# A two-part attention input: key RMS factors as token columns, and the rotary half swap as a DMA

## The chip, the cores and the metric

The kernel runs on one core of one Trainium2 chip. The metric is the device time in microseconds of that core for one execution. The time before is 2725.86 us, the median of 3 runs (2725.54 to 2731.17).

## What is computed

A latent sequence of 512 tokens and a context of 256 tokens, width 1024, go through four blocks in fp32: a hybrid block (mLSTM and short convolution) with an MLP, an attention block with an MLP, and two more blocks of pooling, spatial gating and a gated feed-forward. The change is in the input of the attention block, which is, cut to what matters:

```python
px = hx @ w_in                                   # hx: 512 latent tokens, hc: 256 context tokens
qx = apply_axial_rope(rms_norm(heads(px[..., :nq], 16), q_g), cos, sin)
kx, vx = kv(px[..., nq:])                        # kv: k = rms_norm(heads(k, 4), k_g), v as it is
kx = apply_axial_rope(kx, cos, sin)
kc, vc = kv(hc @ w_in[:, nq:])
k_all = concatenate([kc, kx]);  v_all = concatenate([vc, vx])      # 768 keys, 4 heads of 64

def rms_norm(x, g):  return x * rsqrt(mean(x * x, axis=-1) + EPS) * g
def _rotate_half(part, cs, sn):                  # of the first and of the second 32 channels of a head
    p1, p2 = part[..., :16], part[..., 16:]
    return concatenate([p1 * cs - p2 * sn, p2 * cs + p1 * sn])
```

## The kernel before

Activations lie channel-major: 128 channels on the partitions (two heads of 64), tokens along the free axis, NT = 768 = NC + NX = 256 context + 512 latent. Weights come as a stream of tiles, 128 partitions by 1024 columns (512 KB each). Tile t goes through four buffers (t % 4): SP issues its load once tile t - 4 is used (`load`, line 351), ACT writes the upper part `Whi` (`split_hi`, line 977), DVE the rest `Wlo` (`split_lo`, line 1465). `product` on TensorE (lines 417 to 430) waits for `Wlo`, and for the PSUM bank G[t % 2] to be freed by the evacuation of tile t - 2, then runs 8 times 3 matmuls for each part of the tokens; tiles of keys and values cover all 768 tokens, those of the queries the 512 latent ones.

The attention input has 12 tiles (t = 0 to 11 from T_ATT): two of values, two of keys (n = 0, 1), eight of queries (n = 2 to 9, n = t - 2). Each engine has its own written-out loop over t (TensorE 797, ACT 1299, DVE 2045), and within a loop everything runs in program order. ACT and DVE both begin step t with the split of tile t + 2.

- Keys: ACT copies the product to T (1317) and squares it (1321). TensorE multiplies all 768 tokens by a block of ones (`k_stats`, 771), which puts the sum of squares of a head on each of its channels. ACT takes the root over 128x768 (1332), DVE the reciprocal over 128x768 (`k_finish`, 2025), then normalizes to QN (2026) and copies the context part to AK (2029).
- Queries: ACT squares from PSUM (1324) and copies to T with the gain (1326). `q_stats` (780) puts the sums into columns of B4, a column for each head and 128 tokens; their root (1335) and reciprocal QR (2063) are taken once for all queries, and QR enters the softmax as its scale.
- Rotation: `qk_rotate` (784 to 795) on TensorE multiplies the latent part by the constant matrix `rotate`, which swaps the halves of 16 channels and sets the sign, into B6. `qk_turn` (2031 to 2041) on DVE forms x * cos (2038), swapped x * sin (2040) and their sum (2041) into AK or AQ, and counts `qk_ready`. T has two buffers: ACT may write that of tile n once `qk_ready` shows that n - 2 is turned (1315).

Behind the loop TensorE runs `scores_of(0)` (831), DVE takes `top(0)`, `top(1)` (2070), ACT exponentiates (`weigh`, 1344), and TensorE runs the next scores and `turn_probs` (847), which waits for `qk_ready` 10. `spread_sums` (857) shows the form of matmul that spreads a token column over 64 partitions.

Of the kernel before, what the change touches and what calls it, by code (L numbers as in the profile page):

```python
# [7 lines left out]
ALU = mybir.AluOpType  # L8
ACT = mybir.ActivationFunctionType
AX = mybir.AxisListType  # L10
# [91 lines left out]
def build(nc, xin, cvec, wstream, adaw, firstw, vecs_d, consts_d, rope_d, poolw_d, sguw_d, rows_d, out):  # L102
    ctx = ExitStack()
    with ctx:
# [78 lines left out]
        QR = sb("QR", [P, 64], where=att)  # L183
        p5 = ExitStack()
# [3 lines left out]
        RT = sb("RT", [P, NX], where=p5)  # L188
        p5.close()
# [47 lines left out]
        def ps(bank, a, b):  # L237
# [31 lines left out]
        qk_sq, qk_stat, qk_std, qk_n, rot_done, qk_ready, qr_ready, qg_ready = map(  # L269
            sem, ("qk_sq", "qk_stat", "qk_std", "qk_n", "rot_done", "qk_ready", "qr_ready", "qg_ready"))  # L270
# [65 lines left out]
        def _(sp):  # L336
# [41 lines left out]
            stream(T_ATT + 4, T_S)  # L378
# [37 lines left out]
        def _(pe):  # L416
# [349 lines left out]
            def k_stats(n):  # L766

                pe.wait_ge(qk_sq, n + 1)
                wait(pe, qk_std, n)
                for a, b in parts(FULL):  # L770
                    last = pe.matmul(ps(B4, a, b), blockones, SQ[:, n % 2, a:b], start=True, stop=True)
                last.then_inc(qk_stat, 1)

# [10 lines left out]
            def qk_rotate(n):  # L784

                if n < 2:
                    pe.wait_ge(qk_n, n + 1)
                else:
                    freed(pe, At(T_ATT + 2 + n))
                wait(pe, qk_ready, n - 1)  # L790
                if n == 0:
                    pe.wait_ge(turn_used, 6)
                src_ = QN if n < 2 else T
                pe.matmul(B6[:, NX * (n % 2):NX * (n % 2 + 1)], rotate, src_[:, n % 2, NC:NT], start=True,
                          stop=True).then_inc(rot_done, 1)

            for t in range(N_ATT):
                rng = FULL if t < 4 else LAT
                if t == 0:
                    first_products(At(T_ATT), src, FULL, src_ready, At(8 * S_N2))  # L800
                elif t > 1:
                    product(At(T_ATT + t), src, rng)
                if 1 <= t < 3:
                    turn(4 + t - 1, 0, TT)
                if 3 <= t < 5:
                    k_stats(t - 3)
                if t >= 5:
                    q_stats(t - 3)
                if 4 <= t < 6:
                    qk_rotate(t - 4)  # L810
                if t >= 5:
                    qk_rotate(t - 3)
            q_stats(9)
            qk_rotate(9)
# [157 lines left out]
        def _(act):  # L972
# [326 lines left out]
            for t in range(N_ATT):  # L1299
# [7 lines left out]
                else:  # L1307
# [20 lines left out]
                    if 1 <= n < 3:  # L1328
                        a, b = FULL
                        act.wait_ge(qk_stat, n)  # L1330
                        wait(act, qk_n, n - 1)
                        act.activation(RS[:, a:b], ps(B4, a, b), ACT.Sqrt, scale=1.0 / HD,
                                       bias=VEC[:, VEC_AT["eps"]:VEC_AT["eps"] + 1]).then_inc(qk_std, 1)
# [120 lines left out]
        def _(dve):  # L1454
# [566 lines left out]

            def k_finish(n):

                dve.wait_ge(qk_std, n + 1)
                link(dve.reciprocal(RS[:, :], RS[:, :]))
                dve.scalar_tensor_tensor(out=QN[:, n, :], in0=T[:, n, 0:NT], scalar=vec("k_g"), in1=RS[:, :],
                                         op0=ALU.mult, op1=ALU.mult).then_inc(qk_n, 1)
                dve.wait_ge(qk_n, n + 1)
                dve.tensor_copy(AK[:, n, 0:NC], QN[:, n, 0:NC])

            def qk_turn(n):
                wait(dve, qk_ready, n)
                if n < 2:
                    dst, x_ = AK[:, n, NC:NT], QN[:, n, NC:NT]
                else:
                    dst, x_ = AQ[:, n - 2, :], T[:, n % 2, NC:NT]
                    freed(dve, At(T_ATT + 2 + n))
                link(dve.tensor_tensor(RT[:, :], x_, ROPE[:, 0, :], ALU.mult))
                dve.wait_ge(rot_done, n + 1)
                link(dve.tensor_tensor(dst, B6[:, NX * (n % 2):NX * (n % 2 + 1)], ROPE[:, 1, :], ALU.mult))  # L2040
                dve.tensor_tensor(dst, dst, RT[:, :], ALU.add).then_inc(qk_ready, 1)


            dve.tensor_scalar(small[:, 0:1], vec("q_g"), HD ** -0.5, None, ALU.mult).then_inc(qg_ready, 1)
            for t in range(N_ATT):
                split_lo(At(T_ATT + t + 2))
                if 1 <= t < 3:
                    n = 4 + t - 1
                    dve.wait_ge(turned, n + 1)
                    dve.tensor_copy(AV[:, :, (n - 4) * P:(n - 3) * P],  # L2050
                                    B6[:, 0:NT].rearrange("p (i c) -> p i c", c=P)).then_inc(turn_used, 1)
                if t == 4:
                    dve.wait_ge(late_in, 16)
                if 3 <= t < 5:
                    if t == 4:
                        qk_turn(0)
                    k_finish(t - 3)
                if t == 5:
                    qk_turn(1)
                if t >= 5:  # L2060
                    qk_turn(t - 3)
            dve.wait_ge(qk_std, 3)
            dve.reciprocal(QR[:, :], QR[:, :]).then_inc(qr_ready, 1)
            qk_turn(9)
# [28 lines left out]
            top(1)  # L2093
            for n in range(2 * AH):
# [365 lines left out]
```

## Time and profile before

The trace is of one execution, taken by the hardware profiler.

| | before |
|---|---|
| median of the runs | 2725.86 us |
| the profiled execution, its device time | 2728.78 us |
| its span in the trace | 2727.1 us |
| TensorE busy | 2624.9 us (96%) |
| VectorE busy | 1631.4 us (60%) |
| ScalarE busy | 958.7 us (35%) |
| GpSimd busy | 96.3 us (4%) |
| mean granted TensorE clock | 0.981 |

Times in the trace count from the start of its span. Matmul records overlap, since matmuls are pipelined: what one costs is the distance between starts, not its own length. An fp32 matmul shows as two records. The chain of work that ended last is followed back from the last instruction: each piece is what released the next one. The granted clock is a share of 2.4 GHz: 1.00 is 2.4 GHz, 0.50 is 1.2 GHz.

### The profile page before, as it was taken

Reading aid. Unit: us, or ns where it says so; the run is one execution under the profiler, and the core shown is the slowest. Engines: PE = TensorE matmul, PEld = TensorE weight load, DVE = VectorE, ACT = ScalarE, POOL = GpSimd, SP = SyncE. Lnnn points to the kernel's source line nnn. Section 1 sums busy time; section 2 is a strip of 40 time slices with the busy share of each in tenths; the row PEclk is TensorE's granted clock in tenths of the full one; section 3 lists DMA queues with packets and bytes.
Section 4 is the critical chain, followed back from the end, with each engine's and each line's share of the span. In section 5 each row is a group of like instructions: output and inputs, shape, how many; then the busy total and the mean of one; then the engine's idle time right before and its main releaser. Section 6 shows DMA issues by size and latency. Waiting matters only on the chain.

```text
span 2727.1 us, 35868 instructions
## 1 busy us (share of the span) xinstructions
PE 2624.9 (96%) x13720; PEld 2169.0 (80%) x13720; DVE 1631.4 (60%) x2534; ACT 958.7 (35%) x1405; POOL 96.3 (4%) x185
## 2 busy tenths in 40 slices
PE   7999998999999989899999999989999989899997
PEld 6888887888888877568788888878888778788886
DVE  4877646454546546664755565676566766644446
ACT  2323523222212232674422233353232453532224
POOL 0000000000000000000000000000001000000000
PEclk9999998999999989999999999999999999999998
DMA  6342322333334312001445554234546522233332
GB/s 242 124 139 86 116 78 70 109 108 108 111 110 130 118 49 68 1 1 55 155 147 162 162 187 126 77 101 145 164 149 190 164 81 80 76 93 95 98 94 85
DMA packets 82634, 303.43 MB, mean 111 GB/s; under 512 B 9168, under 2 KB 11344, under 8 KB 81488
## 3 DMA queue, kind: packets, MB, share of 16 engines
q1 hardware_dynamic: 56448, 206.82, 24.0%
q0 software_dynamic: 26064, 94.91, 11.0%
q8 instruction: 85, 1.39, 0.2%
q14 instruction: 37, 0.30, 0.0%
HBM read 299.60 MB, written 2.10 MB: 111 GB/s over the span
## 4 chain that ended last, share of the span: by engine, by line
PE 53%; DVE 5%; ACT 2%; issue 1%; DMA 1%; SPq 0%; ACTq 0%; DVEq 0%
PE G L427 12%; PE G L428 12%; PE G L429 12%; PE G L454 3%; PE G L455 3%; PE G L456 3%; PE B L871 1%; PE G L831 1%; PE G L503 1%; PE G L505 1%; DVE X L1723 1%; PE G L504 1%; PE B L847 1%; DVE T L1720 1%; ACT PR L1344 1%
## 5 line engine op out<-in xcount | busy, mean ns | idle before, releaser
L977 ACT ACTIVATE Whi<-Wraw 128x1024 fp32r<-128x1024 f32 x357 | 374.9, 1051 | 492.3 <-DMA Wraw<-wstream_dram 467.3
L1465 DVE TENSOR_TENSOR Wlo<-Wraw,Whi 128x1024 fp32r<-128x1024 f32 x357 | 436.3, 1222 | 120.7 <-ACT Whi L977 120.1
L427 PE MATMUL G<-h_hi,Whi 128*128 128x512 f32 (+1 forms) x1040 | 372.8, 358 | 2.8 <-DVE Wlo L1465 2.8
L429 PE MATMUL G<-h_hi,Wlo 128*128 128x512 f32 (+1 forms) x1040 | 367.1, 353 | 0.0
L428 PE MATMUL G<-h_lo,Whi 128*128 128x512 f32 (+1 forms) x1040 | 366.9, 353 | 0.0
L427 PE MATMUL G<-hs_hi,Whi 128*128 128x512 f32 x768 | 307.2, 400 | 2.6 <-DVE Wlo L1465 1.7
L428 PE MATMUL G<-hs_lo,Whi 128*128 128x512 f32 x768 | 303.9, 396 | 0.0
L429 PE MATMUL G<-hs_hi,Wlo 128*128 128x512 f32 x768 | 303.8, 396 | 0.0
L429 PE MATMUL G<-hid_hi,Wlo 128*128 128x512 f32 (+1 forms) x792 | 290.8, 367 | 0.0
L427 PE MATMUL G<-hid_hi,Whi 128*128 128x512 f32 (+1 forms) x792 | 290.7, 367 | 0.0
L428 PE MATMUL G<-hid_lo,Whi 128*128 128x512 f32 (+1 forms) x792 | 290.5, 367 | 0.0
L427 PEld LDWEIGHTS G<-h_hi,Whi 128*128 128x128 f32 x1040 | 196.6, 189 | 37.8 <-issue 5.9
L1547 DVE SCALAR_TENSOR_TENSOR X<-G,MOD,X 128x256 f32<-128x256 f32 (+1 forms) x112 | 69.8, 653 | 259.9 <-PE G L429 197.9
L428 PEld LDWEIGHTS G<-h_lo,Whi 128*128 128x128 f32 x1040 | 196.5, 189 | 30.6 <-issue 2.2
L1480 DVE SCALAR_TENSOR_TENSOR Araw<-Araw,CB 128x1024 f32<-128x1024 f32 x180 | 219.0, 1219 | 2.9 <-DMA Araw<-adaw_dram 2.9
L429 PEld LDWEIGHTS G<-h_hi,Wlo 128*128 128x128 f32 x1040 | 196.3, 189 | 29.7
L427 PEld LDWEIGHTS G<-hs_hi,Whi 128*128 128x128 f32 x768 | 144.4, 188 | 38.7 <-DVE Wlo L1465 3.4
L428 PEld LDWEIGHTS G<-hs_lo,Whi 128*128 128x128 f32 x768 | 144.5, 188 | 35.4 <-issue 1.0
L429 PEld LDWEIGHTS G<-hs_hi,Wlo 128*128 128x128 f32 x768 | 144.3, 188 | 35.3
L428 PEld LDWEIGHTS G<-hid_lo,Whi 128*128 128x128 f32 x792 | 148.5, 188 | 27.6
L429 PEld LDWEIGHTS G<-hid_hi,Wlo 128*128 128x128 f32 x792 | 148.5, 188 | 27.5
L427 PEld LDWEIGHTS G<-hid_hi,Whi 128*128 128x128 f32 x792 | 148.6, 188 | 27.5
(387 smaller groups left out, 4397.2 us busy)
## 6 DMA issues: line engine op xcount, KB each, us to landing
Wraw<-wstream_dram SPq DMA_DIRECT2D x357, 512.0 KB, 3.7
Araw<-adaw_dram POOLq DMA_DIRECT2D x180, 512.0 KB, 4.0
FIRST<-firstw_dram SPq DMA_DIRECT2D x4, 1536.0 KB, 23.0
X<-xin_dram SPq DMA_DIRECT2D x4, 1536.0 KB, 11.3
out_dram<-X SPq DMA_DIRECT2D x16, 128.0 KB, 1.7
ROW<-rows_dram SPq DMA_DIRECT2D x2, 768.0 KB, 6.2
CB<-cvec_dram SPq DMA_DIRECT2D x2, 512.0 KB, 5.5
CB<-cvec_dram POOLq DMA_DIRECT2D x1, 512.0 KB, 4.5
```

The lines of the kernel that those rows point to most:

```text
L427: pe.matmul(o, wh, hi[:, a:b], start=(k == 0), stop=False)
L428: pe.matmul(o, wh, lo[:, a:b], start=False, stop=False)
L429: last = pe.matmul(o, wl, hi[:, a:b], start=False, stop=(k == kt - 1))
L454: pe.matmul(o, wh, hi[:, a:b], start=(nth == 0), stop=False)
L455: pe.matmul(o, wh, lo[:, a:b], start=False, stop=False)
L456: last = pe.matmul(o, wl, hi[:, a:b], start=False, stop=(nth == kt - 1))
L503: pe.matmul(o, wh, hi[:, a:b], start=first, stop=False)
L504: pe.matmul(o, wh, lo[:, a:b], start=False, stop=False)
L977: act.activation(Whi[:, t % 4, :], Wraw[:, t % 4, :], ACT.Copy).then_inc(w_hi, 1)
L1465: dve.tensor_tensor(Wlo[:, t % 4, :], Wraw[:, t % 4, :], Whi[:, t % 4, :].bitcast(F32), ALU.subtract).then_inc(w_lo, 1)
L1480: last = dve.scalar_tensor_tensor(out=products, in0=Araw[:, n % 2, :], scalar=1.0, in1=CB[:, v, :], op0=ALU.mult, op1=ALU.mult, accum_out=o)
L1547: last = dve.scalar_tensor_tensor(out=X[:, m, a:b], in0=ps(G[t % 2], a, b), scalar=MOD[:, par, v, gate * 8 + m:gate * 8 + m + 1], in1=X[:, ...
```

## The change

1. `k_stats` puts the sums of squares of the keys into columns of B4 (12 columns for each key tile: 6 blocks of 128 tokens by 2 heads), as `q_stats` does. ACT's root and DVE's reciprocal then work on 128x12 (KR). A new `k_spread` on TensorE spreads the columns over the channels of their head by 12 small matmuls with the identity into B6, one step later; DVE's `k_finish` reads them there.
2. `qk_rotate` is gone. SP copies the latent part of T (or QN) to SWAP by eight DMAs of 16 partitions each, a group g from the group g ^ 16. The sign is put into the sine table once (`signed_sine`).
3. The DMAs are written into SP's program between the loads of the weight tiles, with their waits, and DVE's `qk_turn` runs one step later (n = t - 4 instead of n = t - 3); the last, `qk_turn(9)`, comes behind `top(0)` and `top(1)`.

```diff
+            def swap_halves(n):
+                if n < 2:
+                    sp.wait_ge(qk_n, n + 1)
+                else:
+                    sp.wait_ge(tile_free[(T_ATT + 2 + n) % 2], (T_ATT + 2 + n) // 2 + 1)
+                wait(sp, qk_ready, n - 1)
+                x_ = (QN if n < 2 else T)[:, n % 2, NC:NT]
+                for g in range(0, P, 16):
+                    sp.dma_start(SWAP[g:g + 16, n % 2, :], x_[g ^ 16:(g ^ 16) + 16, :]).then_inc(swapped[n % 2], 16)
+
+            for t in range(4, N_ATT + 3):
+                load(At(T_ATT + t))
+                for n in {7: (0,), 8: (1, 2), 9: (3, 4)}.get(t, (t - 5,) if t > 9 else ()):
+                    swap_halves(n)
+            stream(T_ATT + N_ATT + 3, T_S)
...
 def k_stats(n):
-                for a, b in parts(FULL):
-                    last = pe.matmul(ps(B4, a, b), blockones, SQ[:, n % 2, a:b], start=True, stop=True)
+                for i in range(TT):
+                    at = 64 + 2 * TT * n + 2 * i
+                    last = pe.matmul(B4[:, at:at + 2], SQ[:, n % 2, blk(i)], blockones[:, 0:P:HD], start=True, stop=True)
+            def k_spread(n):
+                pe.wait_ge(kr_ready, n + 1)
...
+                for i in range(TT):
+                    for e in range(2):
+                        last = pe.matmul(ps(B6, i * P, (i + 1) * P)[HD * e:HD * (e + 1), :],
+                                         KR[:, n, 2 * i + e:2 * i + e + 1].to_broadcast([P, HD]), ident, start=True,
+                                         stop=True)
+                last.then_inc(k_spread_done, 1)
...
-                pe.matmul(B6[:, NX * (n % 2):NX * (n % 2 + 1)], rotate, src_[:, n % 2, NC:NT], start=True,
-                          stop=True).then_inc(rot_done, 1)
...
+                if 4 <= t < 6:
+                    k_spread(t - 4)
                 if 3 <= t < 5:
                     k_stats(t - 3)
                 if t >= 5:
                     q_stats(t - 3)
-                if 4 <= t < 6:
-                    qk_rotate(t - 4)
-                if t >= 5:
-                    qk_rotate(t - 3)
             q_stats(9)
-            qk_rotate(9)
...
+            def k_invert(n):
+                dve.wait_ge(qk_std, n + 1)
+                dve.reciprocal(KR[:, n, :], KR[:, n, :]).then_inc(kr_ready, 1)
 def k_finish(n):
-                dve.wait_ge(qk_std, n + 1)
-                link(dve.reciprocal(RS[:, :], RS[:, :]))
-                dve.scalar_tensor_tensor(out=QN[:, n, :], in0=T[:, n, 0:NT], scalar=vec("k_g"), in1=RS[:, :],
-                                         op0=ALU.mult, op1=ALU.mult).then_inc(qk_n, 1)
-                dve.wait_ge(qk_n, n + 1)
-                dve.tensor_copy(AK[:, n, 0:NC], QN[:, n, 0:NC])
+                dve.wait_ge(k_spread_done, n + 1)
+                for dst, a, b in ((AK[:, n, 0:NC], 0, NC), (QN[:, n, NC:NT], NC, NT)):
+                    last = dve.scalar_tensor_tensor(out=dst, in0=T[:, n, a:b], scalar=vec("k_g"), in1=ps(B6, a, b),
+                                                    op0=ALU.mult, op1=ALU.mult)
+                last.then_inc(qk_n, 1)
...
-                dve.wait_ge(rot_done, n + 1)
-                link(dve.tensor_tensor(dst, B6[:, NX * (n % 2):NX * (n % 2 + 1)], ROPE[:, 1, :], ALU.mult))
+                dve.wait_ge(swapped[n % 2], 128 * (n // 2 + 1))
+                link(dve.tensor_tensor(dst, SWAP[:, n % 2, :], ROPE[:, 1, :], ALU.mult))
...
+            def signed_sine():
+                dve.wait_ge(late_in, 16)
+                link(dve.tensor_reduce(small[:, 1:2], rotate, AX.X, ALU.add, negate=True))
+                link(dve.tensor_scalar(ROPE[:, 1, :], ROPE[:, 1, :], small[:, 1:2], None, ALU.mult))
...
-                if t == 4:
-                    dve.wait_ge(late_in, 16)
+                if t == 2:
+                    signed_sine()
+                if 4 <= t < 6:
+                    k_finish(t - 4)
                 if 3 <= t < 5:
-                    if t == 4:
-                        qk_turn(0)
-                    k_finish(t - 3)
-                if t == 5:
-                    qk_turn(1)
-                if t >= 5:
-                    qk_turn(t - 3)
+                    k_invert(t - 3)
+                if t in (5, 6):
+                    qk_turn(t - 5)
+                if t >= 6:
+                    qk_turn(t - 4)
+            qk_turn(8)
             dve.wait_ge(qk_std, 3)
             dve.reciprocal(QR[:, :], QR[:, :]).then_inc(qr_ready, 1)
-            qk_turn(9)
...
             top(0)
             top(1)
+            qk_turn(9)
```

## Rows read from the trace of the kernel before

**Rows 1.** The page: chain that ended last, share of the span by engine.

```profile
PE 53%; DVE 5%; ACT 2%; issue 1%; DMA 1%; SPq 0%; ACTq 0%; DVEq 0%
```

**Rows 2.** Windows: us, each engine's busy time (instructions), PEclk, DMA share, GB/s.

```profile
1036.00:1038.00 2.00, 0.84 (x9) 0.75 (x7) 1.97 (x2) 0.00 (x0) 0.00 (x0) 1.00 0.37 55
1038.00:1040.00 2.00, 1.24 (x2) 0.73 (x3) 1.97 (x3) 1.21 (x3) 0.00 (x0) 0.50 0.52 207
1092.00:1094.00 2.00, 0.00 (x0) 0.00 (x0) 1.80 (x4) 1.16 (x3) 0.00 (x0) 1.00 0.00 0
```

**Rows 3.** Chain that ended last, at the second key tile: start us, us, what.

```profile
1032.79 4.87 DVE RS L2025
...
1037.69 1.03 DVE QN L2026
...
1038.76 3.78 PE B L794 x4
1042.54 0.43 PE G L427
```

**Rows 4.** Timeline of TensorE: start us, us, engine line op, tiles, xcount [idle before].

```profile
1020.56 1.45 PE L771 MATMUL B<-SQ,CON 128*128 128x256 f32 x4
...
1078.49 0.95 PE L780 MATMUL B<-CON,SQ 128*128 128x2 f32 x8
1079.30 1.10 PE L794 MATMUL B<-T,CON 128*128 128x512 f32 x2
1079.84 0.80 PE L427 MATMUL G<-h_hi,Whi 128*128 128x512 f32 x1
1080.48 0.40 PE L428 MATMUL G<-h_lo,Whi 128*128 128x512 f32 x1
...
1085.85 0.95 PE L780 MATMUL B<-CON,SQ 128*128 128x2 f32 x8
```

**Rows 5.** Waits between 1020 and 1092: engine, line <- releaser: total us, times, longest.

```profile
PE B L794 <- DVE QN L2026: 2.4, 2, 1.9
```

**Rows 6.** Timeline of DVE from the last rotation into the attention.

```profile
1089.66 0.63 DVE L2038 TENSOR_TENSOR RT<-T,ROPE 128x512 f32<-128x512 f32 x1
...
1091.66 0.95 DVE L2070 TENSOR_REDUCE NM<-G 128x1 f32<-128x768 f32 x1
...
1095.63 0.96 DVE L2070 TENSOR_REDUCE NM<-B 128x1 f32<-128x768 f32 x1 [1.76 <-PE G L831]
```

**Rows 7.** Timeline of TensorE: a spread of eight token columns.

```profile
1116.46 1.04 PE L857 MATMUL B<-CON,ZR 128*64 128x128 f32 x16
```

**Rows 8.** Timeline of SP: DMAs that it issues back to back.

```profile
4.32 0.62 SPq L346 DMA_DIRECT2D X<-xin_dram  x1
...
2202.62 0.33 SPq L384 DMA_DIRECT2D POW<-poolw_dram  x1
2202.99 0.43 SPq L385 DMA_DIRECT2D SW<-sguw_dram  x1
```

**Rows 9.** The page, DMA issues: xcount, KB each, median us from issue to landing.

```profile
Wraw<-wstream_dram SPq DMA_DIRECT2D x357, 512.0 KB, 3.7
...
out_dram<-X SPq DMA_DIRECT2D x16, 128.0 KB, 1.7
...
POW<-poolw_dram SPq DMA_DIRECT2D x2, 256.0 KB, 2.6
SW<-sguw_dram SPq DMA_DIRECT2D x2, 256.0 KB, 3.0
```

**Rows 10.** Timelines of ACT and DVE in a query step.

```profile
1078.69 0.60 ACT L1324 ACTIVATE SQ<-G 128x512 f32<-128x512 f32 x1 [5.23 <-PE G L429]
...
1079.76 1.06 ACT L977 ACTIVATE Whi<-Wraw 128x1024 fp32r<-128x1024 f32 x1
...
1081.85 1.22 DVE L1465 TENSOR_TENSOR Wlo<-Wraw,Whi 128x1024 fp32r<-128x1024 f32 x1
1082.99 0.68 DVE L2038 TENSOR_TENSOR RT<-T,ROPE 128x512 f32<-128x512 f32 x1
```

More of the change, by code:

```diff
@@ L183, in build @@
         QR = sb("QR", [P, 64], where=att)
+        KR = sb("KR", [P, 2, 2 * TT], where=att)
         p5 = ExitStack()
@@ L188, in build @@
         RT = sb("RT", [P, NX], where=p5)
+        SWAP = sb("SWAP", [P, 2, NX], where=p5)
         p5.close()
@@ L268, in build @@
         hsq2_ready, hidhi_ready = map(sem, ("hsq2_ready", "hidhi_ready"))
-        qk_sq, qk_stat, qk_std, qk_n, rot_done, qk_ready, qr_ready, qg_ready = map(
-            sem, ("qk_sq", "qk_stat", "qk_std", "qk_n", "rot_done", "qk_ready", "qr_ready", "qg_ready"))
+        qk_sq, qk_stat, qk_std, qk_n, qk_ready, qr_ready, qg_ready, kr_ready, k_spread_done = map(
+            sem, ("qk_sq", "qk_stat", "qk_std", "qk_n", "qk_ready", "qr_ready", "qg_ready", "kr_ready",
+                  "k_spread_done"))
+        swapped = [sem(f"swapped{i}") for i in range(2)]
         as_done, amax_ready, aexp_done, at_done, at_used_act, at_used_dve, apv_done, ao_hi_ready = map(
@@ L377, in _ @@
             sp.dma_start(ROPE[:, :, :], rope_d).then_inc(late_in, 16)
-            stream(T_ATT + 4, T_S)
+            def swap_halves(n):
[12 more added lines that the diff above has]
+            stream(T_ATT + N_ATT + 3, T_S)
             for l in range(2):
@@ L769, in k_stats @@
                 wait(pe, qk_std, n)
-                for a, b in parts(FULL):
-                    last = pe.matmul(ps(B4, a, b), blockones, SQ[:, n % 2, a:b], start=True, stop=True)
+                for i in range(TT):
+                    at = 64 + 2 * TT * n + 2 * i
+                    last = pe.matmul(B4[:, at:at + 2], SQ[:, n % 2, blk(i)], blockones[:, 0:P:HD], start=True, stop=True)
                 last.then_inc(qk_stat, 1)
+            def k_spread(n):
+                pe.wait_ge(kr_ready, n + 1)
+                if n == 0:
+                    pe.wait_ge(turn_used, 6)
+                wait(pe, qk_n, n)
+                for i in range(TT):
[4 more added lines that the diff above has]
+                last.then_inc(k_spread_done, 1)
             def q_stats(n):
@@ L782, in q_stats @@
                 last.then_inc(qk_stat, 1)
[L784 to L793, printed above, removed]
-                pe.matmul(B6[:, NX * (n % 2):NX * (n % 2 + 1)], rotate, src_[:, n % 2, NC:NT], start=True,
-                          stop=True).then_inc(rot_done, 1)
             for t in range(N_ATT):
@@ L1328, in _ @@
                     if 1 <= n < 3:
-                        a, b = FULL
                         act.wait_ge(qk_stat, n)
-                        wait(act, qk_n, n - 1)
-                        act.activation(RS[:, a:b], ps(B4, a, b), ACT.Sqrt, scale=1.0 / HD,
+                        at = 64 + 2 * TT * (n - 1)
+                        act.activation(KR[:, n - 1, :], B4[:, at:at + 2 * TT], ACT.Sqrt, scale=1.0 / HD,
                                        bias=VEC[:, VEC_AT["eps"]:VEC_AT["eps"] + 1]).then_inc(qk_std, 1)
@@ L2034, in qk_turn @@
                     dst, x_ = AK[:, n, NC:NT], QN[:, n, NC:NT]
+                    dve.wait_ge(qk_n, n + 1)
                 else:
```

## The prediction, made before the changed kernel was seen

> **What bounds the kernel now.** I read the page first. TensorE is the largest term of the chain that ended last [rows 1], so only what lies on TensorE's path counts, and the question is what the attention input costs there. The stretch runs from 1020.56, where the product of the second key tile ends and `k_stats` begins, to 1085.85, where the last query product ends [rows 4]: 65.29 us. Behind it, until DVE's third maximum at 1095.63 [rows 6], the chain goes through DVE. From there on nothing is touched by the change.
>
> The timeline of TensorE gives the price of each piece in a query step, as distances of starts [rows 4]. 23 product matmuls, from the second of a tile at 1080.48 to the next `q_stats` at 1085.85, take 5.37 us, 0.233 each, so a product of 24 takes 5.60. `q_stats` takes 0.81 (1078.49 to 1079.30). `qk_rotate` takes 0.54 to the next start, and the first product matmul behind it takes 0.64 where 0.233 is normal, so a rotation costs 0.54 + 0.41 = 0.95.
>
> The chain [rows 3] shows why the keys cost more. The reciprocal over 128x768 (4.87) and the normalization (1.03) on DVE released the rotation of the key, for which TensorE sat idle 2.4 us in two waits, 1.9 of them in the second [rows 5]. Behind the second wait the windows show the granted clock at 0.50, 1.2 GHz, having been 1.00 while TensorE was busy only 0.84 of 2.00 us [rows 2]. Two rotations took 3.78 instead of 1.9, and the first product matmul behind them 0.43 instead of 0.233 [rows 3]; six ran at that pace. The fall cost 1.9 + 1.2 = 3.1.
>
> **The change part by part.**
>
> *Rotations off TensorE.* Eight stood before 1085.85 and two behind, 0.95 each. In the stretch that is 7.6; the two waits add 2.4 and the clock 3.1. Removed: 13.1.
>
> *`k_stats` as columns.* 6 blocks against 4 in `q_stats`: 0.81 x 6/4 = 1.22. Before, it took about 0.9 + 0.4 for the late first product matmul, 1.3. Two of them: gain 0.2.
>
> *`k_spread`, new.* The nearest row is the same form with 8 matmuls. Its record has 1.04 us [rows 7], part of which overlaps the next, as the 0.95 of `q_stats` stands for a distance of 0.81 [rows 4]. That is 0.90 to 1.04 for 8, 1.35 to 1.56 for 12; I take 1.47, twice 2.94. If they were free the time would be 2.9 lower, which is the bound below; above, I take 12 at 0.25 (one product matmul's pace), 3.0 each. I keep 1.47, since the form is the same. Its input is ready: root and reciprocal of 128x12 follow 1.3 us after `k_stats`, and a product of 5.6 us hides them. Without that cover they would cost these 1.3.
>
> *Restart behind a small matmul.* No row shows a product directly behind `q_stats`. Between 0 and the 0.41 behind a rotation; I take 0.1, since the 0.41 follows 512 moving columns and these have 2. Eight products: 0.8.
>
> TensorE's own path from 1020.56 is then 8 x 5.7 + 2 x 1.22 + 2 x 1.47 + 6 x 0.81 = 55.8, and the last product ends at 1076.4, 9.4 us earlier, provided that nobody makes it wait.
>
> *DVE.* The two long reciprocals and the copies go, and the two halves of `k_finish` cost what one 128x768 costs (1.03 [rows 3]), plus 0.2. `signed_sine` (a 128x128 sum and a 128x512 product, about 1 us by the 0.68 of a 128x512 [rows 10]) lies in an idle time of DVE ahead of the next split and costs nothing; without that cover the split would move 1 us and still have a whole product in hand.
>
> *SP, the part that decides.* Each tile now has eight DMAs and their waits in front of the next weight load. The first of a sequence takes 0.33 and the next starts 0.37 behind it; that next one takes 0.43, with the same gap 0.47; the longest has 0.62, with the gap 0.66 [rows 8]. All those have 128 partitions, these 16, so the bound below is open (0.05, if it goes by descriptors) and above 0.66. I take 0.40, near the lower of the pair, so 3.2 for a tile. For landing, the eight together are 256 KB: between 1.7 (128 KB) and 2.6 (256 KB) [rows 9]; I take 2.0 from the last issue.
>
> Behind the waiting SP stand the weight loads: load n + 6 is issued only when tile n is evacuated and swapped. On the price of an issue the Trainium skill ("DMA: Bandwidth & Descriptors", Anatomy of one DMA) has about 50 ns for the dispatch by a sequencer. No row of this case shows an issue under 0.33, and the row decides. By the skill's figure the loads would not be late and the time would be that of the second case below.
>
> I follow the new loop through. Let E(n) be the time when ACT has evacuated query tile n. A cycle over two tiles is: swap(n) issued 3.2, load 3.7 [rows 9], `split_hi` 1.1 (1.06 [rows 10]), `split_lo` 1.15 (1081.85 to 1082.99), `qk_turn` 2.0 (1089.66 to 1091.66 [rows 6]), ACT's square and copy 1.2 (1.07 from 1078.69 to 1079.76 and 0.1 for the semaphore [rows 10]), 0.1 for a semaphore: 12.45. TensorE needs 2 x (5.7 + 0.81) = 13.0 for two tiles. So it holds, with 0.5 to spare, but starts late. Product 4 ends at 1020.6 + 1.2 + 5.7 = 1027.5; `k_spread(0)` and `k_stats(1)` take 2.7, product 5 ends at 1035.9 and `k_spread(1)` at 1037.3; `k_finish(1)` takes 1.2 and ends at 1038.6. Then come the swap of n = 1 until 1041.9, that of n = 2 until 1045.1 and load 9 behind them (landing 1048.8). The swap of n = 2 lands at 1046.7 (7 issues and 2.0 behind its start), DVE has turned n = 2 1.3 later, at 1048.0, and with ACT's 1.2 E(4) is 1049.2. E(5) lies 5.4 behind it (`split_hi`, `split_lo`, `qk_turn`, ACT: 1.1 + 1.15 + 2.0 + 1.2), and from there every second one follows in 12.4: E(6) = 1061.6, E(8) = 1074.0, and on the odd side E(5) = 1054.6, E(7) = 1067.0, E(9) = 1079.4. TensorE wants E(4) by 1051.2, E(5) by 1057.7, E(6) by 1064.2, E(7) by 1070.7, so no product waits. But `q_stats(9)` wants the last square, at 1078.8 instead of 1077.2. TensorE idles 1.7 us.
>
> *The end.* `scores_of(0)` starts at 1079.7, its first result is there 1.6 later, and `top(0)` runs at 1081.3 instead of 1091.66. The last swap is issued from 1079.5 and lands at 1084.3; `top(1)` ends at 1083.4, so `qk_turn(9)` ends at 1085.7. Before, the third maximum came 3.97 behind the first [rows 6], which would be 1085.3. So it now starts at 1085.7, and the gain is 1095.63 - 1085.7 = 9.9 us. `turn_probs` waits for the same `qk_ready` and moves by the same.
>
> **The rivals.**
>
> *The cover holds whole.* If an issue takes well under 0.37, SP is not in the cycle, the first maximum is at 1076.4 + 1.6 + 1.6 = 1079.6, and the third, behind the turn, at 1083.7 to 1084.0. Gain 11.6 to 11.9, up to 12.5 if restarts are free: 2713.4 to 2714.3. For it: 16 descriptors instead of 128. Against: the 0.33 of every single issue.
>
> *SP becomes the bound.* The issue time enters the chain to the end five times eight, so the gain is 9.9 - 40 x (issue - 0.40): at 0.47 7.1, at 0.66 -0.5 (2726.4). From 0.65 on the change gives nothing.
>
> *The other side: the pieces land one by one.* POW and SW, issued 0.37 apart, land 0.8 apart (2.6 and 3.0 after issue) [rows 8, 9]. If each small DMA occupied the queue that long, a swap would take 6.4 instead of 3.2 and the load behind it would wait with it, which acts like an issue time of 0.80: 9.9 - 16 = -6.1, 2732.0. It decides from about 0.78 (5.5 us slower). For it stands the Trainium skill (same page, Rules for kernel authors): "Two transfers to disjoint partition halves" serialize, and under 64 KB a transfer is mostly overhead; these have 32 KB. Against it: those 0.8 us were for 256 KB of data, eight times as much, so little of it can be a fixed share.
>
> *The clock falls again.* TensorE idles 1.7 us at the end of the input, after sparse matmuls, as it did before the fall [rows 2]. In the other stretch, 1092 to 1094, it did nothing and the clock stayed at 1.00. If it falls: 3.1, gain 6.8, 2719.1.
>
> **How the numbers follow.** The profiled execution ran 2728.78 with a span of 2727.1; less 9.9 its span is 2717.2. Against the median it is 2725.9 - 9.9 = 2716.0, since the profiled run stood 2.9 above it and the gain is in one stage. Chances: forecast (issue 0.37 to 0.47, 2714.8 to 2718.8) 0.50; cover whole 0.15; clock 0.10; SP the bound with 0.47 to 0.70 (2718.8 to 2728) 0.15; one by one 0.10. About 0.2%, 5.5 us, is what a measurement can tell. Faster takes the first three but for 0.02 and a third of the fourth: 0.77, taken as 0.75. Slower 0.10, same 0.15. The range goes from the whole cover, 2713.5, to the zero point of SP as the bound, 2726; it leaves out the one-by-one case and the ends of the others.
>
> **What would show it.** TensorE: `q_stats` followed by L427 in under 0.3 us beyond 0.81, no rotation, no idle time and clock 1.00 between 1020 and 1077; `k_spread` 1.3 to 1.6. SP: eight issues 0.37 to 0.47 apart, landing under 3 us. The last product ends at 1076 to 1077, then an idle time of 1 to 3 us before the last `q_stats`; first maximum at 1081, third at 1085 to 1086. The forecast is wrong if products wait for `Wlo` or the PSUM bank, if a load lands after ACT asks for it by more than in the cycle above, or if the clock is at 0.50 anywhere in the stretch.

## The result, and the profile after

| | before | after |
|---|---|---|
| median of 20 runs each, same chip | 2727.26 us | 2733.05 us |
| ratio, with its 95% interval | | 1.0021 [1.0014, 1.0028] |
| the profiled execution, its device time | 2728.78 us | 2734.78 us |
| its span | 2727.1 us | 2733.1 us |

The change makes the kernel 5.7 us slower (2727.26 x 0.0021), where 9.9 us faster was forecast. The page of after: all engines together have less to do than before, and the time went up.

```profile
span 2733.1 us, 36001 instructions
PE 2622.0 (96%) x13764; PEld 2170.9 (79%) x13764; DVE 1623.6 (59%) x2536; ACT 957.8 (35%) x1405; POOL 96.1 (4%) x185
SWAP<-T SPq DMA_DIRECT2D x64, 32.0 KB, 2.0
```

TensorE is busy 2.9 us less, VectorE 7.8. The timeline of TensorE in after answers [rows 4, 5] (L792 is `k_stats`, L803 `k_spread`, L814 `q_stats`, L447 the first matmul of a product, L849 `scores_of`):

```profile
1021.87 1.40 PE L792 MATMUL B<-CON,SQ 128*128 128x2 f32 x12
1023.12 0.47 PE L447 MATMUL G<-h_hi,Whi 128*128 128x512 f32 x1
...
1028.89 1.53 PE L803 MATMUL B<-CON,KR 128*64 128x128 f32 x24
1030.35 1.50 PE L792 MATMUL B<-CON,SQ 128*128 128x2 f32 x12
...
1053.84 1.05 PE L814 MATMUL B<-CON,SQ 128*128 128x2 f32 x8 [1.70 <-ACT SQ L1342]
...
1070.30 1.87 PE L814 MATMUL B<-CON,SQ 128*128 128x2 f32 x8 [3.24 <-ACT SQ L1342]
1072.03 0.77 PE L447 MATMUL G<-h_hi,Whi 128*128 128x512 f32 x1
...
1086.46 0.95 PE L814 MATMUL B<-CON,SQ 128*128 128x2 f32 x8
1091.38 1.86 PE L814 MATMUL B<-CON,SQ 128*128 128x2 f32 x8 [3.97 <-ACT SQ L1342]
1093.18 2.93 PE L849 MATMUL G<-AK,AQ 64*128 64x512 f32 x8
```

Counted from the end of the second key product (1020.56 before, 1021.87 after; the 1.3 us between lie ahead of the change), the last product ended at +65.29 and now ends at 1086.46, +64.59. Of the forecast 9.4 us only 0.7 came. `q_stats` waits three times for its square, 1.70, 3.24 and 3.97 us. The first two lie ahead of the end of the last product, and behind the second the clock was at half: from 1070.30 to the next `q_stats` at 1080.00 it took 9.70 us, where the same step takes 6.46 at full clock (1080.00 to 1086.46). These 4.9 + 3.2 us, with some 0.4 of slower starts behind waits, are what the last product lost against the +55.98 that the kernels without waits reach below. The third wait comes behind it. The third maximum, which closed the stretch at +75.07 [rows 6], now starts at 1101.56, +79.69: 4.6 us later, and the span is 6.0 longer, 1.3 of it from ahead. So the loss lies in this stretch: 0.7 us gained up to the last product, 5.3 lost between it and the third maximum (15.1 us instead of 9.8).

Who made the square late? The timelines of ACT and DVE ahead of the wait at 1070.30:

```profile
1065.19 1.06 ACT L995 ACTIVATE Whi<-Wraw 128x1024 fp32r<-128x1024 f32 x1 [4.80 <-DMA Wraw<-wstream_dram]
1069.65 0.60 ACT L1342 ACTIVATE SQ<-G 128x512 f32<-128x512 f32 x1 [3.39 <-DVE AQ L2063]
1066.29 1.23 DVE L1482 TENSOR_TENSOR Wlo<-Wraw,Whi 128x1024 fp32r<-128x1024 f32 x1 [7.15 <-ACT Whi L995]
1067.43 0.69 DVE L2060 TENSOR_TENSOR RT<-T,ROPE 128x512 f32<-128x512 f32 x1
```

Each step stands behind the one before: a weight tile lands, ACT splits it at 1065.19 after 4.80 us of waiting, DVE's half of the split begins at 1066.29, the turn of tile 4 behind it in program order at 1067.43, and only then is a buffer of T free for tile 6, so its square starts at 1069.65. TensorE names the square, ACT names the turn, but the first of the chain is a load. The timeline of SP in after says why the load was late (L392 are the swaps, L355 the weight loads):

```profile
1031.64 5.31 SPq L392 DMA_DIRECT2D SWAP<-QN  x8
1037.00 0.57 SPq L355 DMA_DIRECT2D Wraw<-wstream_dram  x1
1040.22 4.94 SPq L392 DMA_DIRECT2D SWAP<-QN  x8
1045.28 4.94 SPq L392 DMA_DIRECT2D SWAP<-T  x8
1050.26 0.58 SPq L355 DMA_DIRECT2D Wraw<-wstream_dram  x1
1050.94 9.98 SPq L392 DMA_DIRECT2D SWAP<-T  x16
1060.97 0.58 SPq L355 DMA_DIRECT2D Wraw<-wstream_dram  x1
1061.65 6.07 SPq L392 DMA_DIRECT2D SWAP<-T  x8
1067.76 0.58 SPq L355 DMA_DIRECT2D Wraw<-wstream_dram  x1
```

From 1040.22 to 1067.76 SP does nothing but issue: five swaps of eight DMAs and two loads between them. A swap takes 5.0 us, 0.63 for each DMA: 0.59 in the median and a gap of 0.04. One issue took 1.64, which is why one swap shows as 6.07. The tile SWAP in after:

```profile
L392 SPq DMA_DIRECT2D SWAP<-T x64: 507/589/1640, 1045.3 to 1096.3; - x64
DMA to landing us min/median/max: 1.9/2.0/3.7
```

The granted clock fell twice, after the second and the third wait. Windows of after, to be held against [rows 2]:

```profile
1066.00:1070.00 4.00, 1.06 (x5) 0.53 (x3) 3.21 (x4) 0.61 (x2) 0.00 (x0) 1.00 0.37 75
1072.00:1074.00 2.00, 2.00 (x6) 1.61 (x7) 1.24 (x2) 0.72 (x1) 0.00 (x0) 0.50 0.25 57
1088.00:1090.00 2.00, 0.00 (x0) 0.00 (x0) 1.93 (x4) 0.00 (x0) 0.00 (x0) 1.00 0.23 52
1094.00:1096.00 2.00, 2.00 (x8) 0.67 (x4) 0.18 (x1) 0.90 (x1) 0.00 (x0) 0.50 0.27 67
```

### The profile page after: what moved, and what is told of

It reads as the page before. It is cut to its first block, busy times and chain, and to the rows that moved or that the text cites. A ratio compares the mean times of both kernels' runs of the same rounds, so it can differ in the third digit from the quotient of the medians.

```text
span 2733.1 us, 36001 instructions
## 1 busy us (share of the span) xinstructions
PE 2622.0 (96%) x13764; PEld 2170.9 (79%) x13764; DVE 1623.6 (59%) x2536; ACT 957.8 (35%) x1405; POOL 96.1 (4%) x185
## 3 DMA queue, kind: packets, MB, share of 16 engines
q0 software_dynamic: 26064, 94.91, 11.2%
## 4 chain that ended last, share of the span: by engine, by line
PE 87%; DVE 6%; ACT 3%; issue 2%; DMA 1%; SPq 1%; DVEq 0%; ACTq 0%
PE G L447 20%; PE G L449 20%; PE G L448 20%; PE G L474 5%; PE G L475 5%; PE G L476 5%; PE B L640 2%; SPq L392 1%; PE G L849 1%; PE B L889 1%; PE G L523 1%; PE G L524 1%; PE G L525 1%; DVE X L1740 1%; PE B L865 1%
## 5 line engine op out<-in xcount | busy, mean ns | idle before, releaser
L447 PE MATMUL G<-h_hi,Whi 128*128 128x512 f32 (+1 forms) x1040 | 371.1, 357 | 2.8 <-DVE Wlo L1482 2.8
L447 PE MATMUL G<-hs_hi,Whi 128*128 128x512 f32 x768 | 306.4, 399 | 2.6 <-DVE Wlo L1482 1.7
L447 PE MATMUL G<-hid_hi,Whi 128*128 128x512 f32 (+1 forms) x792 | 290.6, 367 | 0.0
L447 PEld LDWEIGHTS G<-h_hi,Whi 128*128 128x128 f32 x1040 | 197.6, 190 | 35.6 <-issue 3.7
L447 PEld LDWEIGHTS G<-hs_hi,Whi 128*128 128x128 f32 x768 | 144.0, 187 | 38.7 <-DVE Wlo L1482 3.4
L447 PEld LDWEIGHTS G<-hid_hi,Whi 128*128 128x128 f32 x792 | 148.5, 188 | 27.5
```

The source lines that it names most:

```text
L447: pe.matmul(o, wh, hi[:, a:b], start=(k == 0), stop=False)
```

## The experiments

Two theories stood against each other. SP: the eight issues cost 0.63 us each and stand ahead of the next load, so their number and their place set the time. Clock: the time goes with the fall of TensorE's clock at the handover to the attention, whatever caused the waits. Beside them, the parts of the change were tried alone. The medians are of 20 runs for after, of 11 for e1, e2, e5, e9 and e10, and of 5 for the others. Local times below count from the end of the second key product, as above, and are of one profiled execution each. The last product's time is where it ends.

| kernel | median, us | before, same chip | ratio [95%] | last product | third maximum |
|---|---|---|---|---|---|
| before | | | | +65.29 | +75.07 |
| after | 2733.05 | 2727.26 | 1.0021 [1.0014, 1.0028] | +64.59 | +79.69 |
| e1_columns | 2731.68 | 2727.54 | 1.0015 [1.0005, 1.0024] | +61.99 | +79.21 |
| e2_load_first | 2723.55 | 2727.54 | 0.9987 [0.9978, 0.9996] | +57.94 | +71.27 |
| e3_four | 2718.12 | 2727.54 | 0.9965 [0.9951, 0.9978] | +55.98 | +66.15 |
| e4_one | 2717.78 | 2727.54 | 0.9965 [0.9952, 0.9979] | +55.98 | +63.68 |
| e5_columns_in_step | 2725.11 | 2728.74 | 0.9992 [0.9983, 1.0001] | +62.85 | +74.00 |
| e6_sixteen | 2781.16 | 2728.74 | 1.0194 [1.0180, 1.0208] | +93.46 | +124.23 |
| e7_four_first | 2716.60 | 2728.74 | 0.9959 [0.9945, 0.9972] | +55.98 | +64.22 |
| e8_four_first_busy | 2718.80 | 2728.74 | 0.9965 [0.9951, 0.9978] | +55.98 | +63.68 |
| e9_after_busy | 2732.01 | 2727.46 | 1.0017 [1.0008, 1.0026] | +61.69 | +77.54 |
| e10_rows_eight | 2731.22 | 2727.46 | 1.0016 [1.0007, 1.0025] | +62.26 | +78.68 |
| e11_rows_four_first | 2717.70 | 2727.46 | 0.9964 [0.9950, 0.9977] | +53.08 | +63.92 |
| e12_four_first_again | 2717.64 | 2727.46 | 0.9961 [0.9948, 0.9975] | +55.98 | +64.73 |
| e13_rows_busy | 2715.55 | 2728.31 | 0.9948 [0.9935, 0.9962] | +53.14 | +61.63 |
| e14_four_busy_again | 2718.20 | 2728.31 | 0.9960 [0.9946, 0.9973] | +55.98 | +63.67 |

**The columns alone.** The key factors as columns, with the rotation left on TensorE.

```diff
-            for t in range(4, N_ATT + 3):
-                load(At(T_ATT + t))
-                for n in {7: (0,), 8: (1, 2), 9: (3, 4)}.get(t, (t - 5,) if t > 9 else ()):
-                    swap_halves(n)
-            stream(T_ATT + N_ATT + 3, T_S)
+            stream(T_ATT + 4, T_S)
...
+            def qk_rotate(n):
...
+                pe.matmul(turned_half(n), rotate, src_[:, n % 2, NC:NT], start=True,
+                          stop=True).then_inc(rot_done, 1)
```

> Only the first part of the change: key factors as columns and their spread; the rotation stays a matmul on TensorE, one step later than before (n = t - 4), with the last turn behind the second maximum. Theory (the columns gain, the DMAs lose): the two waits for the key (2.4 us) and the clock's fall (3.1) go, two spreads of 1.46 come, one rotation moves behind the last product: 3.4 less up to the last product, 0.5 given back behind it, so 2.9 us faster than before. Rival (the sparse matmuls of the columns cost the clock or delay the key): 2 us or more slower than before.

The last product ended at +61.99, as expected, and yet the kernel is 4.1 us slower than before by the ratio, where 2.9 faster was expected. I had put each rotation one step later, to match after's turns. At the end that gives another wait, 2.26 us, and the last two rotations at half clock. Timeline of TensorE in e1_columns (L827 is the rotation):

```profile
1085.96 1.87 PE L815 MATMUL B<-CON,SQ 128*128 128x2 f32 x8 [2.26 <-ACT SQ L1360]
1087.69 3.76 PE L827 MATMUL B<-T,CON 128*128 128x512 f32 x4
```

So this run says nothing of the columns, but of the handover: 3.3 us saved in the products were lost there more than twice over. The next kernel puts the rotations of the later query tiles (n = 5 and up) back into the steps where before had them, and the last turn ahead of the first maximum. Against e1, on TensorE:

```diff
-                if t in (5, 6):
-                    qk_rotate(t - 5)
-                if t >= 6:
-                    qk_rotate(t - 4)
+                for n in {5: (0,), 6: (1, 2), 7: (3, 4)}.get(t, (t - 3,) if t > 7 else ()):
+                    qk_rotate(n)
```

> As e1, but with the rotations of the queries from the fifth on back in the step they had before (n = t - 3) and the last turn ahead of the first maximum, as before. In e1 the last square waited for the turn of tile 7, whose rotation stood behind the last product, and TensorE idled 2.3 us and fell to 1.2 GHz. Theory (the columns gain, e1 lost by its order at the end): 65.3 us up to the last product become 62.8, nothing is given back behind it: 2.5 us faster than before. Rival (the columns lose by themselves): 2 to 4 us slower than before, as e1.

The last product came at +62.85, as expected. By the ratio the gain is 2.2 us, of the expected size, though its interval reaches past 1. What the columns give here is that the key's long wait goes. In the profiled execution only 1.1 of the 2.4 us is left at the third maximum (+74.00 against +75.07): the third scores ran at half clock there, which had not been expected.

**Order of the load.** One change in SP's program against after: each load goes ahead of the swaps that it stood behind (from n = 5 on the load of tile n + 6 ahead of the swap of tile n).

```diff
-            for t in range(4, N_ATT + 3):
+            for t in range(4, 9):
                 load(At(T_ATT + t))
...
+            for n in range(5, 10):
+                if n + 6 < N_ATT + 3:
+                    load(At(T_ATT + n + 6))
+                swap_halves(n)
```

> The changed kernel with one thing moved in SP's program: the load of weight tile n + 6 stands ahead of the eight DMAs of query n instead of behind them. Theory (SP's issue time, 8 x 0.63 = 5.0 us, stands between the evacuation of tile n and load n + 6): the load leaves that cycle, the last query tile is evacuated about 9 us earlier than in the changed kernel, and the time is 3 to 4 us below that of before. Rival 1 (the landing of the small DMAs, or the turn one step later, sets the pace): within 1 us of the changed kernel, 5 to 6 above before.

As expected: 2723.55, 9.5 us below after by the medians (3.5 by the ratio below before), with the same DMAs. The swaps land as in after (2.0 us in the median) and the turns stand in the same step, so neither explains the difference. The order by itself doesn't tell SP's issue time from transfers that hold up a load behind them, but the load was hardly held there: in after ACT's split began 3.9 to 4.2 us after the issue of such a load, against a landing of 3.7 in the median before [rows 9].

**Number of issues.** The channels of a head are permuted on the host so that the partner lies 32 partitions away; four DMAs of 32 partitions then do the same swap. On the chip only the count that DVE waits for changes with it.

```diff
-                for g in range(0, P, 16):
-                    sp.dma_start(SWAP[g:g + 16, n % 2, :], x_[g ^ 16:(g ^ 16) + 16, :]) ...
+                for g in range(0, P, 32):
+                    sp.dma_start(SWAP[g:g + 32, n % 2, :], x_[g ^ 32:(g ^ 32) + 32, :]) ...
```

> The changed kernel with the channels of a head laid out so that the partner of a channel is 32 partitions away instead of 16: four DMAs of 32 partitions for a swap instead of eight of 16, same bytes, same place in SP's program. Theory (time goes by the number of issues, 0.63 each): 2.5 us for a swap instead of 5.0, less than the 3.7 up to which the load is in time, so TensorE waits nowhere and the gain against before is 11 to 12 us. Rival (an issue costs by its rows or bytes): 4 x 1.25, as slow as the changed kernel, 5 to 6 above before.

9.5 us faster than before by the ratio, short of the 11 to 12 expected, which the interval (6.0 to 13.4) still holds: the last `q_stats` waits 0.92 us, and the third scores run at half clock. With twice the bytes in each DMA the issue still takes 0.59, so a swap takes 2.4 us. The tile SWAP in e3_four:

```profile
L392 SPq DMA_DIRECT2D SWAP<-T x32: 507/590/595, 1040.9 to 1079.9; - x32
```

One DMA of 128 partitions, which leaves the half swap out (it copies only), shows what less than four would be worth.

```diff
+                sp.dma_start(SWAP[:, n % 2, :], x_).then_inc(swapped[n % 2], 16)
```

> The changed kernel with one DMA of 128 partitions in place of the eight. It copies each channel to its own place, so the half swap is left out and the rotated values are other ones; everything else is the same. Theory (number of issues): nothing left of SP's share; 11.5 to 12 us below before, hardly better than with four. Rival 1 (landing, 2.0 us, and the turn one step later): no gain from fewer issues, 5 to 6 above before.

The same time as with four, 9.5 and not the 11.5 to 12 expected, and an issue of 0.47. The tile SWAP in e4_one:

```profile
L391 SPq DMA_DIRECT2D SWAP<-T x8: 464/465/471, 1038.6 to 1075.5; - x8
```

And sixteen DMAs of 8 partitions, in the other direction.

```diff
+                for g in range(0, P, 8):
+                    sp.dma_start(SWAP[g:g + 8, n % 2, :], x_[g ^ 16:(g ^ 16) + 8, :]) ...
```

> The changed kernel with sixteen DMAs of 8 partitions for each swap: twice the issues, the same bytes. Theory (0.63 for each issue, SP is the bound): a swap takes 10 us of SP instead of 5, nine of them in a row with one load each: 9 x 5 = 45, less what SP idled in the changed kernel, about 39 above it and 44 above before, 2772. Rival 1 (time goes by bytes or by landing): within 2 us of the changed kernel. Rival 2 (the clock of TensorE is the main loss): under 10 above the changed kernel.

52.9 us slower than before by the ratio: 0.625 an issue, 10.7 a swap, and one `q_stats` that waits 16.27 us. That is 9 more than the 44 expected; about 5 of them are the issue, 0.665 with its gap instead of 0.63 (9 x 16 x 0.035), the rest I did not trace. The tile SWAP, and TensorE's timeline, in e6_sixteen:

```profile
L392 SPq DMA_DIRECT2D SWAP<-T x128: 624/625/652, 1052.1 to 1140.6; - x128
...
1066.35 1.87 PE L814 MATMUL B<-CON,SQ 128*128 128x2 f32 x8 [16.27 <-ACT SQ L1342]
```

One, four, eight and sixteen issues for each tile give -9.5, -9.5, +5.7 and +52.9 us by the ratios, and an issue takes 0.47 to 0.63 whatever it moves. With one and with four the last product ends at the same +55.98, so SP is not in the cycle; with eight and sixteen it is. Together with the order, that settles the cause for SP's issues. What an issue spends its time on, no run shows.

**Both mendings together.** Four DMAs and the load first; run twice.

```diff
+                if n + 6 < N_ATT + 3:
+                    load(At(T_ATT + n + 6))
+                swap_halves(n)
...
+                for g in range(0, P, 32):
```

> e3 and e2 together: four DMAs of 32 partitions and the load of tile n + 6 ahead of the swap of n. In e3 ACT still waited 2.5 us in all for weight loads and TensorE 0.9 for the last square. Theory (issue time and order are the whole loss): neither is left, the last product ends 56 us behind the key's product, gain against before 10 to 12 us. Rival (the rest of e3's loss lies in the turn one step later): as e3, 9 to 9.5.

> e7 once more, on the chip of e11, to compare the two: 10 to 12 us below before.

11.2 and 10.6 us faster than before by the ratios. TensorE waits for nothing up to the last product, at +55.98, and from n = 5 on the load of tile n + 6 no longer waits for the swap of tile n.

**The clock.** Dummy matmuls, which nobody reads, fill TensorE's waits: two behind the first scores in e8; in e9 the kernel after itself with 1, 3 and 6 ahead of three `q_stats` and 2 behind the scores.

```diff
+            for _ in range(2):
+                pe.matmul(B6[:, 0:NX], ident, CON[:, 0:NX], start=True, stop=True)
             for n in range(2 * AH):
```

> e7 with two matmuls (128x512 of constants by the identity, read by nobody) behind the first scores, where TensorE waits 2.5 us for ACT: about 1.9 us of work in an idle time. In e3 the granted clock was 0.50 for the next scores and transposes and the third maximum came 5.35 behind the first; in e4 it was 1.00 and 4.2. Theory (the idle time lets the clock fall): the clock stays at 1.00, third maximum 4.2 behind the first, and the time is 0 to 1.2 us below e7, since e7 falls only in some executions. Rival (the clock has nothing to do with it, or the extra matmuls delay the scores): equal to e7 or up to 1 us above.

```diff
+                fill({7: 1, 9: 3}.get(t, 0))
                 if t >= 5:
                     q_stats(t - 3)
+            fill(6)
             q_stats(9)
```

> The changed kernel with matmuls of constants that nobody reads (128x512, about 0.95 us each) where TensorE waited: 1 ahead of q_stats(4), 3 ahead of q_stats(6), 6 ahead of q_stats(9), 2 behind the first scores. It separates the price of the waits from that of the clock that fell behind them. Theory: the waits stay, since SP sets them; the fall between 1070 and 1077 (3.2 us) only moves into the last wait, but the one at the end (1.0 in q_stats, 1.4 in the scores, 1.2 to the third maximum) is on the path, so 2.5 to 3.5 us below the changed kernel, 2 to 3 above before. Rival (the clock costs nothing that SP has not already cost): equal to the changed kernel.

In e8 the clock stayed at 1.00 and the third maximum came 0.5 earlier than in e7. The time does not show it: the median is 2.2 us above that of e7, where 0 to 1.2 below was expected, and the five runs of e8 spread over 9.8 us. In e9 it stayed at 1.00 from 1020 to 1102, and the kernel is still slower than before, 4.6 us instead of 5.7. The expected gain of 2.5 to 3.5 over after was too high. The third maximum came at +77.54 rather than +79.69. The turn of the last tile then holds the path, and it hangs on SP, whose last swap starts at +69.81 in e9 and at +70.06 in after; TensorE waits for that turn. Timeline of TensorE in e9_after_busy (L873 is `turn_probs`):

```profile
1096.54 0.63 PE L873 MATMUL B<-CON,PR 128*128 128x128 f32 x4 [1.59 <-DVE AQ L2072]
```

The clock theory alone falls: with no fall at all four fifths of the loss remain (4.6 of 5.7), and even the lower end of its interval, 2.2 us, is a loss. How the loss splits in the medians is not sharp, since the intervals of e9 and after overlap; the local times carry it.

**The DMA part alone.** The key factors as rows again, as before had them, on top of after, and on top of the mended kernel.

```diff
-                for i in range(TT):
-                    last = pe.matmul(B4[:, at:at + 2], SQ[:, n % 2, blk(i)], blockones[:, 0:P:HD], start=True, stop=True)
+                for a, b in parts(FULL):
+                    last = pe.matmul(ps(B4, a, b), blockones, SQ[:, n % 2, a:b], start=True, stop=True)
...
-                    k_spread(t - 4)
```

> Only the second part of the change: the swap by eight DMAs as in the changed kernel, the key factors again over 128x768 rows with the 4.9 us reciprocals on DVE, no spread. Theory (SP is the bound, the columns only move when it starts): the second key is ready about 1.5 us earlier, SP's row of swaps starts that much earlier, so 4 to 5 us above before. Rival (the DMAs need the columns to pay): 8 us or more above before.

> e7 (four DMAs of 32 partitions, load ahead of the swap) with the key factors over rows again. Theory (with the rotation off TensorE nobody there waits for DVE's long reciprocals, and the two spreads are 2.9 us of TensorE for nothing): 2.5 to 3 us below e7, 13.5 to 14.5 below before. Rival (the reciprocals still delay the keys or the splits): level with e7 or above it.

With eight DMAs, 4.4 us slower than before, as expected: the loss is that of the DMAs, and the columns neither cause nor cure it. With four, the last product came 2.9 us earlier than in e12, as expected (55.98 - 53.08, the two `k_spread`), but the time did not: 2717.70 against 2717.64, and by the ratio 9.8 us below before instead of the 13.5 to 14.5 expected. Behind a wait of 0.65 the first scores ran at half clock, and the third maximum stood only 0.8 ahead. Timeline of TensorE and a window of e11_rows_four_first:

```profile
1076.03 2.38 PE L855 MATMUL G<-AK,AQ 64*128 64x512 f32 x6
...
1078.00:1082.00 4.00, 1.49 (x6) 0.64 (x6) 2.97 (x6) 1.88 (x3) 0.00 (x0) 0.50 0.51 164
```

If that is the reason, dummies in e11 should bring the 2.9 us out. The next kernel has rows, four DMAs, the load first and dummies (one ahead of the last `q_stats`, two behind the scores), and beside it the same with columns (e8 again):

```diff
+            fill(1)
             q_stats(9)
...
             scores_of(0)
+            fill(2)
```

> e11 with one matmul of constants ahead of q_stats(9) and two behind the first scores. In e11 the last product ended 53.1 us behind the key's (56.0 in e12), 2.9 earlier as expected, but its time was level with e12: the clock stood at 0.50 already in the first scores, where e12 still had 1.00. Theory (the clock took most of the 2.9): with the idle times filled the clock stays at 1.00, the third maximum comes 61 us behind the key's product instead of 63.9, and the time is 1.5 to 3 us below e11 and 12 to 13 below before. Rival (the last turn, or something else at the handover, holds it): third maximum at 63 to 64, time as e11.

> e8 once more, on the chip of e13: clock at 1.00 up to the third maximum, which comes 63.7 behind the key's product; 10 to 12 us below before. Theory: e13 is 2 to 3 below it.

e14 is as expected. In e13 the clock is 1.00 and the third maximum comes at 1082.98, +61.63, where 61 was expected; the gain is above the 12 to 13 expected. Window and timeline of DVE in e13_rows_busy:

```profile
1078.00:1082.00 4.00, 3.40 (x14) 1.42 (x12) 3.24 (x7) 2.87 (x5) 0.00 (x0) 1.00 0.56 156
...
1082.98 0.95 DVE L2110 TENSOR_REDUCE NM<-B 128x1 f32<-128x768 f32 x1
```

At 2715.55 it is 14.2 us faster than before by the ratio, and its median is 2.6 us below that of e14 on the same chip. The intervals of these two against before overlap, so the medians alone don't carry it; the local times have 2.0 us (61.63 against 63.67), of the 2.8 at the last product.

## Why the prediction was wrong

**What held.** The prices on TensorE, by distances of starts: `k_stats` 1.25 (1.22 forecast), `k_spread` 1.46 (1.47), `q_stats` 0.81, a restart behind `q_stats` 0.06 (6.47 from one `q_stats` to the next in e3, less 0.81 and 5.60; 0.1 forecast). `signed_sine` lay in idle time, a DMA of a swap landed 2.0 after its issue in the median, the turn takes 2.1. TensorE's own path of 55.8 is the +55.98 of e3, e4, e7 and e14. Up to 1050 there was no idle time and a clock of 1.00. The case in which the cover holds whole put the third maximum at 63.1 to 63.4 (1083.7 to 1084.0); e8 and e14, with four DMAs, have 63.68 and 63.67.

**The step that failed** is the price of one issue on SP. I took 0.40, near the lower of a pair [rows 8]. It was 0.63 with the gap, close to the 0.66 that I had named as the upper end, and that turned 3.2 us for a swap into 5.0. The pair stands a second time in the trace of before, at 1665, and there the second issue took 0.74 instead of 0.43. Line 385 in before:

```profile
L385 SPq DMA_DIRECT2D SW<-sguw_dram x2: 432/587/742, 1665.5 to 2203.0; - x2
```

So one row was no basis for the low end, and the sum turned on it. That the copy is dearer because it goes from SBUF to SBUF is not shown: a weight load from DRAM, 0.33 by itself (1022.06 in after), took 0.57 to 0.58 directly behind a swap. Fewer partitions don't make an issue cheaper either: the first DMA of a swap took 0.51 with 16 or 32 partitions, the only one of e4 0.47 with 128.

**The second step** is the slope. I let the issue time enter five times eight, because I had the swap of tile 4 wait for E(4). At 0.63 nothing waits: swaps 1, 2, 3, 4 and 5 stand in one row on SP [SP's timeline above], then 7, then 9, seven times eight. At 0.40 that chain gives 1091.93 - 1021.87 - 6 x 1.84 = 59.0 for the start of the last swap, level with the 58.9 of my sum, so the two cannot be told apart there. Above, an estimate of the gain is 9.9 - 56 x (issue - 0.40), and its zero lies at 0.58, not at 0.65. For 0.63 it gives a loss of 3.0, where my rival "SP becomes the bound", right in its mechanism, still gives a gain of 0.7; e9, in which the clock never fell, has its third maximum 2.5 behind before. e6 also rules out five: a swap costs 5.7 us more than in after and the third maximum comes 44.5 later, nearly eight swaps. The cycle over two tiles was right in form: 12.45 + 8 x 0.23 = 14.3 against the 14.6 between the swaps of 7 and 9 in after.

**The third step** is that the clock's fall stood as a case of its own. Late loads make TensorE wait, and behind a wait it fell, so the two come together. Its price was 79.69 - 77.54 = 2.1 us, less than the 3.1 I had, since SP's pace hid the rest. Loss by the two: 2.5 + 2.1 = 4.6, the shift of the third maximum in after. The median of all runs has 5.7; the last 1.1 I can't place. Two slips of addition don't bear on this: the chance of faster sums to 0.78, not 0.77, and the whole cover with free restarts gives 12.7 (11.9 + 0.8), not 12.5.

The rival "one by one" gave 2732.0, close to the measured time, by a mechanism that did not happen: the landing stayed at 2.0 us in the median, and the price was paid on SP. That its number is near is luck. The Trainium skill ("DMA: Bandwidth & Descriptors", Rules for kernel authors) asks for one large transfer instead of many small ones. Going from eight to four, e3 took a step that way and was 15.2 us faster than after by the ratios, through SP's issue time. The 50 ns that the Trainium skill (same page, Anatomy of one DMA) has for the dispatch stand there for DMAs issued from GpSimd, so they are no price for SP's issues, as the prediction took them. Here those took 0.47 to 0.63 us.

## What to carry to other kernels

Price a DMA by the time that its issuing engine spends on it, and from more than one row, best of issues that follow each other directly; it went here by the number of DMAs and hardly by their size. Before putting issues into a queue that also feeds the weights, add them up along the whole queue and put the load first: the same work in another order was worth 9 us. Issuing the swaps from another engine was not tried. Where a gain lies ahead of a handover between engines, look at the clock behind the new wait; a few dummy matmuls in the idle time kept it up. With them a gain of 2.8 us ahead of the handover left 2.0 at the third maximum, without them one of 2.9 left 0.8; each of these is from one execution.

## What the runs showed of the hardware

- Issuing a copy from SBUF to SBUF took SP, in a row of such issues, 0.625 us with 8 partitions (e6) and 0.59 with 16 (after) or 32 (e3), each with a gap of about 0.04. The first of a row took 0.51 with 16 or 32, a single one 0.47 with 128 (e4). A weight load took 0.33 by itself and 0.57 to 0.58 directly behind a swap (after).
- The granted clock fell behind waits of 3.24 and 3.97 us in after, of 2.26 in e1 and of 0.65 in e11, and did not behind 1.70 in after. Behind a wait of 3.06 us at the same place, the one ahead of the third scores, the first matmul took 0.66 in before and 1.19 in e5. Behind 2.52 at that place it was 0.66 in e7, with the next at 0.93, and 1.09 in e12, which is the same kernel. So the length of the wait alone doesn't tell whether it falls; what decides it was not found. With the waits filled it stayed at 1.00 in e8, e9, e13 and e14.
- ACT's split began 3.9 to 4.2 us after the issue of a load that stood behind a swap in after (1060.97 to 1065.19, 1067.76 to 1071.67), against a landing of 3.7 in the median before [rows 9].
